# Eleven weight slots in place of nine, and a gather by float32 products, in a two-layer decoder trunk with routed experts

## The reference, cut to what matters

```python
def moe_swiglu(h, router_w, w_gate, w_up, w_down):
    logits = (xf @ router_w)
    top_logits, top_idx = lax.top_k(logits, TOP_K)          # TOP_K = 2
    gates = softmax(top_logits)
    ...
    # for each expert e, for the tokens that chose it:
    ys = (silu(xb @ w_gate[e]) * (xb @ w_up[e])) @ w_down[e] * gate
    ...
    # summed back at each token's place; x = x + that
```

## Time and profile before

| | |
|---|---|
| median of 3 runs | 1292.83 us |
| the profiled execution | 1290.49 us, span 1288.3 us |
| granted TensorE clock, mean | 0.994 |
| TensorE matmuls busy | 1244.5 us, 97% |
| VectorE busy | 346.4 us, 27% |
| ScalarE busy | 315.8 us, 25% |
| bytes moved, mean rate | 417.62 MB, 324 GB/s |
| chain that ended last | TensorE 80%, DMA 9%, VectorE 5%, ScalarE 3% |

### The profile page before, as it was taken

How to read it: one execution, slowest core, us unless ns; L and a number is a source line. 1 busy time by engine, 2 the same in 40 slices (tenths; PEclk the granted TensorE clock), 3 DMA queues, 4 the chain that set the end, 5 groups by cost and what they waited for, 6 DMA issues and landing times.

```text
span 1288.3 us, 20298 instructions
## 1 busy us (share of the span) xinstructions
PE 1244.5 (97%) x8998; PEld 721.2 (56%) x8998; DVE 346.4 (27%) x682; ACT 315.8 (25%) x695; POOL 0.2 (0%) x4
## 2 busy tenths in 40 slices
PE   7999999999999899999999999999999989999976
PEld 6788999998769534443544453443453344444323
DVE  5678654555577600100010001010001001000100
ACT  5676544445577300100100010010001010001000
POOL 0000000000000000000000000000000000000000
PEclk9999999999999899999999999999999999999999
DMA  9923552465411599999999999999999999999995
GB/s 360 387 82 131 196 196 99 165 229 190 189 66 66 196 381 407 409 413 407 409 413 409 408 394 404 408 408 412 407 411 412 412 406 409 412 408 408 413 408 224
DMA packets 114746, 417.62 MB, mean 324 GB/s; under 512 B 3424, under 2 KB 8160, under 8 KB 102240
## 3 DMA queue, kind: packets, MB, share of 16 engines
q1 hardware_dynamic: 114656, 416.29, 82.5%
HBM read 415.23 MB, written 1.05 MB: 323 GB/s over the span
## 4 chain that ended last, share of the span: by engine, by line
PE 80%; DMA 9%; DVE 5%; ACT 3%; SPq 2%; issue 1%; DVEq 0%; ACTq 0%
PE ps L917 39%; PE ps L932 12%; PE ps L571 6%; PE ps L572 6%; PE ps L573 6%; DMA ring<-moe_g 2%; DMA ring<-moe_u 2%; DMA ring<-moe_d 2%; DMA more_ring<-moe_u 2%; PE ps L963 1%; SPq L511 1%; PE ps L1012 1%; DMA ring<-w_in 1%; DVE xres L1426 1%; DVE scratch L1544 1%
## 5 line engine op out<-in xcount | busy, mean ns | idle before, releaser
L917 PE MATMUL ps<-ring,xgT 128*64 128x512 f32 (+1 forms) x1536 | 309.7, 555 | 11.0 <-DMA ring<-moe_g 6.0
L917 PEld LDWEIGHTS ps<-ring,xgT 128*64 128x64 f32 x1536 | 110.6, 138 | 194.7 <-issue 180.1
L1872 DVE TENSOR_TENSOR hT<-ps,hT 128x512 f32<-128x512 f32 (+3 forms) x32 | 23.7, 741 | 561.6 <-PE ps L917 500.8
L917 PE MATMUL ps<-ring,hidT 128*64 128x512 f32 x736 | 167.5, 597 | 7.4 <-DMA ring<-moe_d 6.7
L1686 DVE TENSOR_TENSOR d_lo<-ring,d_hi 128x1024 fp32r<-128x1024 f32 x82 | 99.7, 1223 | 77.3 <-ACT d_hi L1279 77.1
L1324 ACT ACTIVATE hidT<-ps 128x512 f32<-128x512 f32 (+3 forms) x32 | 20.4, 637 | 402.9 <-PE ps L963 215.2
L1279 ACT ACTIVATE d_hi<-ring 128x1024 fp32r<-128x1024 f32 x82 | 85.9, 1062 | 99.1 <-PE ps L573 99.1
L917 PEld LDWEIGHTS ps<-ring,hidT 128*64 128x64 f32 x736 | 51.1, 137 | 101.3 <-issue 99.7
L571 PE MATMUL ps<-hT_hi,d_hi 128*128 128x256 f32 x352 | 99.7, 283 | 0.0
L573 PE MATMUL ps<-hT_hi,d_lo 128*128 128x256 f32 x352 | 99.6, 283 | 0.0
L572 PE MATMUL ps<-hT_lo,d_hi 128*128 128x256 f32 x352 | 99.6, 283 | 0.0
(11 more groups left out here) (257 smaller groups left out, 1316.8 us busy)
## 6 DMA issues: line engine op xcount, KB each, us to landing
ring<-moe_d SPq DMA_DIRECT2D x46, 2048.0 KB, 22.7
ring<-moe_u SPq DMA_DIRECT2D x45, 2048.0 KB, 23.8
ring<-moe_g SPq DMA_DIRECT2D x41, 2048.0 KB, 25.8
more_ring<-moe_g SPq DMA_DIRECT2D x15, 2048.0 KB, 23.6
more_ring<-moe_u SPq DMA_DIRECT2D x11, 2048.0 KB, 23.7
more_ring<-moe_d SPq DMA_DIRECT2D x10, 2048.0 KB, 20.8
ring<-w_in SPq DMA_DIRECT2D x6, 2048.0 KB, 10.1
ring<-dense_g SPq DMA_DIRECT2D x5, 2048.0 KB, 8.0
```

The lines of the kernel that those rows point to most:

```text
L917: ins = pe.matmul(ps[q * HALF:(q + 1) * HALF, b0, 0:wide], x, w[:, i * cols + q * wide:i * cols + (q + 1) * wide], start=first, stop=last, ...
L1872: nc.vector.tensor_tensor(hid[:, 0:w], ps_flat[:, 2 * CH:2 * CH + w], sig[:, 0:w], ALU.mult).then_inc(dve_done, dve_p.step((g, s, "hid", c)))
```

## The change

`MORE_SLOTS` goes from 2 to 4, so 11 slots serve the experts. The room comes from two places: the mixer constants, `uq` and `ukv` move into a region that is given free after the mixers and over which the expert buffers now lie (only `ident`, `ones`, `rank_tri` and `iota` are kept), and `xn_hi`, `xn_lo` and a separate `pick_gT` are dropped. The normalised tokens stand once, in float32, in `xn`. The gather takes 128x128 blocks of `xn` as the stationary operand and `pick` as the moving one, 16 full float32 products of 128 columns, whose results are already transposed. The copy to `rows` and the transposes go. The constants are loaded by two transfers, and their semaphore is waited for at 32.

```diff
-MORE_SLOTS = 2
+MORE_SLOTS = 4
@@ SP
-                    sp.dma_start(consts[:, P:], cst[:, P:]).then_inc(const_loaded, 16)
+                    sp.dma_start(consts[:, P:], cst[:, P:N_KEPT]).then_inc(const_loaded, 16)
+                    sp.dma_start(mixer_consts[:], cst[:, N_KEPT:]).then_inc(const_loaded, 16)
@@ TensorE, gather(s)
-                    for n in range(2):
-                        dims = slice(n * CH, (n + 1) * CH)
-                        for a in range(TT):
-                            pe.matmul(ps[:, 6 + n, :], pick[:, a, :], xn_hi[:, a, dims], start=a == 0, stop=False,
-                                      skip_group_check=True)
-                        pe.matmul(ps[:, 6 + n, :], pick[:, 0, :], xn_lo[:, 0, dims], start=False, stop=False,
-                                  skip_group_check=True)
...
-                def gathered_T(s, it=None):
-                    pe.wait_ge(act_done, at((g, s, "rows_read"), it))
-                    for k in range(KD):
-                        ins = pe.transpose(ps[:, 6 + k // 4, k % 4 * P:(k % 4 + 1) * P], rows[:, k * P:(k + 1) * P], ident)
+                    for k in range(KD):
+                        for a in range(TT):
+                            ins = pe.matmul(ps[:, 6 + k // 4, k % 4 * P:(k % 4 + 1) * P], xn[:, a, k * P:(k + 1) * P],
+                                            pick[:, a, :], start=a == 0, stop=a == TT - 1, skip_group_check=True)
                         if k % 4 == 3:
                             ins.then_inc(pe_done, pe_p.step((g, s, "gathered", k // 4)))
@@ ScalarE
-                    act.wait_ge(pe_done, at((g, s, "rows", 1), it))
-                    nc.scalar.activation(rows, ps[:, 6:8, :].rearrange("p b n -> p (b n)"),
-                                         ACT.Copy).then_inc(act_done, act_p.step((g, s, "rows_read")))
...
-                nc.scalar.activation(xn_hi[:, a, :], xres[:, a, :], ACT.Copy, scale=stat[:, 4 + a:5 + a])...
+                nc.scalar.activation(xn[:, a, :], xres[:, a, :], ACT.Copy, scale=stat[:, 4 + a:5 + a])...
@@ VectorE
-                xn_low(0)
                 dve.wait_ge(pe_done, at("ranks"))
...
-                    if g == 0 and e == 0:
-                        xn_low(1)
```

More of the change, by code:

```diff
@@ L280, in trunk_program, with sb_stage @@
         ps = ctx.enter_context(nc.psum_tensor("ps", [P, 8, 512], F32))
+        with ExitStack() as trunk:
+            mixer_consts = trunk.enter_context(nc.sbuf_tensor("mixer_consts", [P, N_CONST - N_KEPT], F32))
+            uq = trunk.enter_context(nc.sbuf_tensor("uq", [P, 2, HA * QK], F32))
+            ukv = trunk.enter_context(nc.sbuf_tensor("ukv", [P, HA * (NOPE + HD)], F32))
+            with ExitStack() as stage:
+                def sb_stage(name, shape, dt=F32):
+                    return stage.enter_context(nc.sbuf_tensor(name, shape, dt))
+                with ExitStack() as projection:
+                    in_hT_lo, in_lo, in_hi = (projection.enter_context(nc.sbuf_tensor(n, shape, F32R)) for n, shape in (
+                        ("in_hT_lo", [P, KD, T]), ("in_lo", [P, IN_SPLIT, PIECE]), ("in_hi", [P, IN_SPLIT, PIECE])))
+                mla_T = sb_stage("mla_T", [P, 2 * HA, T])
+                swa_qT = sb_stage("swa_qT", [P, HB // 2, T])
+                swa_kT = sb_stage("swa_kT", [P, T])
+                stick_qT = sb_stage("stick_qT", [P, HC // 2, T])
+                stick_kT = sb_stage("stick_kT", [P, HC // 2, T])
+                stick = sb_stage("stick", [P, HC, SEG])
+                sb_stage("beside", [P, 2304])
+                cols = sb_stage("cols", [P, TT, IN_COLS])
+                scratch = sb_stage("scratch", [P, 8 * SEG])
+                mla_v = sb_stage("mla_v", [P, TT, HA * HD])
+            with ExitStack() as stage:
+                def sb_stage(name, shape, dt=F32):
+                    return stage.enter_context(nc.sbuf_tensor(name, shape, dt))
+                hid_hi = sb_stage("hid_hi", [P, 2, 4 * T], F32R)
+                hid_lo = sb_stage("hid_lo", [P, 2, 4 * T], F32R)
+                d_hi_01 = sb_stage("d_hi_01", [P, 2, PIECE], F32R)
+                d_lo_01 = sb_stage("d_lo_01", [P, 2, PIECE], F32R)
+                hT_hi = sb_stage("hT_hi", [P, KD, T], F32R)
+                hT_lo = sb_stage("hT_lo", [P, KD, T], F32R)
+                d_hi_23 = sb_stage("d_hi_23", [P, 2, PIECE], F32R)
+                d_lo_23 = sb_stage("d_lo_23", [P, 2, PIECE], F32R)
         with ExitStack() as stage:
@@ L285, in sb_stage @@
                 return stage.enter_context(nc.sbuf_tensor(name, shape, dt))
[L286 to L309, removed]
@@ L310, in trunk_program @@
-        with ExitStack() as stage:
-            def sb_stage(name, shape, dt=F32):
-                return stage.enter_context(nc.sbuf_tensor(name, shape, dt))
+            more_ring = sb_stage("more_ring", [P, MORE_SLOTS, UNIT])
             xgT = sb_stage("xgT", [P, KD, GROUP])
             hidT = sb_stage("hidT", [P, 2, BIG * 2 * P])
-            pick = sb_stage("pick", [P, TT, GROUP], F32R)
+            pick = sb_stage("pick", [P, TT, GROUP])
             pick_g = sb_stage("pick_g", [P, TT, 2 * P])
[L317 to L320, removed]
+            y = sb_stage("y", [P, BIG * T])[:, :]
@@ L338, in trunk_program @@
         sig, hid = hT_flat[:, 0:768], hT_flat[:, 768:1536]
-        rows, y = xn[:, 0, :], xn[:, 1, 0:BIG * T]
+        pick_gT = hT_flat[:, 1536:2048]
         ps_flat = ps[:, :, :].rearrange("p b n -> p (b n)")
```

37 lines of the change are left out of this document (11 added, 26 removed).

## The result

The changed kernel takes 1274.36 us, the median of 4 runs (1271.22 to 1275.39). The kernel before took 1292.59 us (4 runs, 1292.15 to 1293.09). The ratio is 0.9855, with a 95% interval from 0.9843 to 0.9868. The profiled execution took 1271.22 us, with a span of 1269.4 us.

What follows compares the result with a forecast made beforehand. Expert weight transfers were taken as the bound, with TensorE 19.1 us behind. The stream's gain of 12.8 us less 0.6 us at the full ring gave -12.2 us, forecast 1280.6 us, 8-in-10 range 1277.8 to 1286.

Steps and rivals of the forecast that it cites:

- A 2 MB unit (2.097 MB) so takes 5.12 us: Expert weight stream: transfer time of one unit, taken from the steady 410 GB/s of the kernel before.
- What costs nothing: Constants' second transfer, pick_gT and y changing places, and SP's two earlier issues: claimed to add no time.
- Two more slots: Start of expert stream: units 9 and 10 issued at about 428, carrying 10.2 us of transfers into the gap.
- The first gather: Chain before unit 0: gather of 3.5 us, unit 0 starting at 444.2, 2.4 us earlier than before.
- Rival (a): First gather and unit 0: TensorE stays at its lower clock, gain only 8.3 us, 1284.5 us; chance 0.09.
- The gathers inside the experts: Seven later gathers: 3.6 us each, 0.55 us dearer, 3.9 us together on TensorE, hidden beside the transfers.
- TensorE's distance from being the bound: Last unit's start: TensorE alone 1257.8, transfers 1262.6, so transfers stay last with 4.8 us between them.
- The full ring: Behind big experts 1 and 2, SP waits for slots: 0 to 1.5 us of gain lost, 0.6 taken.
- Rival (b): Full ring gives the head start back: only 7.6 of 12.8 us survive, 1285.2 us; chance 0.12.
- Rival (c): Stream start: added slots bring no earlier issue, only the chain's 1.6 to 3.3 us remain, 1290.4 us; chance 0.03.
- rival (d): Inner gathers make TensorE the bound: at 8.1 us each, 1310 us; chance 0.06 at any price above break-even.

Runs made afterwards that it cites:

- e1_misaligned: The changed kernel with 416 bytes of padding ahead of the expert buffers, putting more_ring 416 bytes past a multiple of 512; 1279.13 us, ratio 0.9906.
- e3_before_aligned: The kernel before with 96 bytes of padding ahead of more_ring, so its two slots start on a multiple of 512; 1285.51 us, ratio 0.9953.
- e2: The changed kernel with 416 bytes of padding ahead of the expert buffers and MORE_SLOTS back at 2 (nine slots, new gather); 1289.19 us, ratio 0.9984.
- e4_all_aligned: The changed kernel with 128 bytes of padding ahead of ring and 128 ahead of the expert buffers, all slots on multiples of 256; 1267.65 us, ratio 0.9808.
- e9: The changed kernel with the 384-byte tile stat allocated ahead of ring, so both slot arrays start on multiples of 512; 1268.64 us, ratio 0.9820.
- e5: The changed kernel with its four more_ring slots at 0, 64, 256 and 448 bytes past a multiple of 512; 1273.91 us, one execution.
- e11: The kernel before with 384 bytes of padding ahead of ring and 224 ahead of more_ring, all nine slots on multiples of 512; 1277.94 us, ratio 0.9893.
- e8: e9 with the seven inner gathers over the first 128 tokens only, 8 products for 16; 1260.49 us, ratio 0.9765.

## Why the prediction was wrong

- **The step that failed** is in its first paragraph: "A 2 MB unit (2.097 MB) so takes 5.12 us". I read the rate of the kernel before as a property of the chip and carried it over to the changed one. It was the rate of slots that all began badly; 60 of the 168 units now go to `more_ring` (36 before), and its slots take 0.11 to 0.3 us less than those of `ring`. The windows put this at 6.6 us, the landings at 6.3, and e1_misaligned against the changed kernel at 0.51%, 6.6 us. (e3_before_aligned gives 6.1 us for its 36 units.)
- **The step where it should have been seen** is "What costs nothing". There I listed what moves in order and in waits, and left out what moves in memory, though the diff allocates `more_ring` in another place. With the earlier trace rows alone the size could not be had, since no slot of that trace lay well. But the move could have been named, with a sentence of its own and a wider low end; as it was, the range ended 3.4 us above the result.
- *Two more slots*: right. Units 9 and 10 are issued at 428, and the gap gives 12.9 us at unit 11, for 12.8 forecast. e2 to e1 gives 10.1 us for the two slots, for 10.2 forecast.
- *The first gather*: right in the sum, by luck. Unit 0 starts at 444.30 (444.2). But the router ends 0.7 us later than in the execution before (its product at L847 at 437.14, where the same product stood at 436.48), the gather takes 3.81 us (3.5), and against these 1.0 us the clock was back at its upper level before the gather, where I had added 0.9 us, half the price of the lower one. Rival (a) did not come about in the profiled execution. In e4_all_aligned's profile its first half did: the clock was at 0.50 from 433 to 443.4, and unit 0 starts at 446.81, the very 446.8 of the rival. The clock had then risen, and unit 11 lands only 2.0 us later than in e9 (458.01 for 456.03), where rival (a) took 4.5 us from the gain. The four executions at a mean clock of 0.995 suggest that this is common; where their clock fell, no trace shows.
- *The gathers inside the experts*: right. 3.67 us (3.6). From the start of the unit ahead to the start of the unit behind, 7.48 us against 5.75, and 3.48 against 4.60 for the next, where the transposes were: 0.61 us more each (0.55).
- *TensorE's distance from being the bound*: wrong, and hidden by luck. I took TensorE's own end as the last unit's start less all waits, and got 1257.8 for the changed kernel. In e9 it runs through without a wait for weights and starts the last unit at 1250.33, from a unit 0 at 443.84; from 444.30 that is 1250.8, 7 us earlier than forecast. In the changed kernel the faster stream used up what I had not counted, so 4.8 us of waits were left as forecast; with the forecast's stream, e1_misaligned, 10.0 are left. The sum of the waits understates what TensorE has to spare. Why is open; that the kernel before runs at a clock of 0.50 for 3.4 us from 1255 us on, among the waits, may be a part.
- *The full ring*: mis-sized. Measured by the rate around it, 700 to 800 lost 60 x 3/410 + 1.7 = 2.1 us before and 60 x 9/415 + 40 x 34/415 = 4.6 us now, 2.5 us of the gain, where I took 0.6. At the rate that I had assumed the step was right: e1_misaligned loses 40 x 19/409 = 1.9 us in 760 to 800, for 1.7 before. The rate holds at 410 in 700 to 760 there, so with the forecast's stream nothing of the gain was lost, within my 0 to 1.5. It is the faster stream that runs into the full ring. Rival (b) is the same loss, which it priced at 12.8 - 7.6 = 5.2 us; half of that was met.
- *Rival (c)* fell with the issues at 428.01 to 429.49, and *rival (d)* with the gather's 3.67 us.
- The gains of e1 (12.1 us) and of the placement (6.6 us by the windows and by e1) come to 18.7, for the measured 18.2; nothing larger than the spread of a measurement is left over.

Two things stay open. The well placed units take 4.89 us (4 KB pieces) where their neighbours lie badly (e3, e5) and 4.97 us where all lie well (e4, e9, e11). The changed kernel has both: its four slots of `more_ring`, filled one after another behind those of `ring`, take 4.89, 4.91, 4.97 and 4.97 us. So the larger gain goes to the first two units behind badly placed ones, and the lasting one is from 5.11 to 4.97; this is also why 36 units gave nearly as much as 60. What the second limit is, no run was made on. And I did not measure whether it is the write to the slot or something that goes with its address; that the start of the slot decides it, e5_mixed shows.

## What to carry to other kernels

In a kernel that is bound by transfers, compute the start of every buffer that a large DMA fills, before and after a change, and treat an array that moves as part of the change, even if no instruction moves; here two pads of together 608 bytes gave more (1.1%) than 32 KB of additional slots (0.8%), per partition. When two bounds are near one another, state how far apart they are and what each edit does to that distance: the dearer gathers (4.3 us in all) were free while TensorE had 4.8 us of waits, and no longer once the transfers were faster. Measure that distance by an experiment that makes one side cheaper or dearer: the sum of the waits put it 5 us too low. A steady GB/s at a DMA share above 1.0 says that the engines are full, not that they cannot move more in the same time.

## What the runs showed of the hardware

- A 2 MB transfer in 4 KB pieces takes 5.05 to 5.12 us where the destination starts off a multiple of 256 B, and 4.89 to 4.98 us where it starts on one (4.97 in a row of such transfers); in 8 KB pieces 4.95 to 5.00 and 4.86 to 4.90 (4.96 over the nine such units of `more_ring` in e11); in 2 KB pieces 5.33 to 5.41 and 4.97 to 5.13. The steady rate is 410 GB/s with no slot well placed and 421 with all. The DMA share reads 1.02 in both.
- The 16 DMA engines do not keep step. In the changed kernel the time from the first engine's end to the last one's is 0.4 us at unit 8, 5.1 at unit 60, 2.1 at unit 80, behind the stretch in which SP waits for slots, and 7.7 at the last unit (1248.45 and 1256.17; 1268.22 and 1275.30 before). Each unit waits for the slowest. Over all runs it is 5.5 to 8.3 us at the last unit; with every slot well placed 5.5 to 6.0 (e4, e9, e11) and 6.8 (e8).
- A full float32 product of 128x128 by 128 columns takes 0.23 us (3.67 us for 16), in two records.
- With the same instructions, TensorE's clock is at 0.50 for 3.4 us before the first gather in one execution and for 10.2 us in another (433.5 to 436.9 in the changed kernel, 433.2 to 443.4 in e4, whose pads move no instruction); unit 0 starts 2.5 us later in the second.
